# Compressed logits behind four slices of the recurrent inputs, and a reordered start and end of the first attention

## What is computed

```python
# first layer: h = rmsnorm(x) @ w_in, split into z, xbc, dt, q, k, v, z_sb, gates
y   = ssd_scan(silu(conv(xbc)), dt, ...)
for each block of 128 queries and each of 16 heads:          # stick-breaking
    logits   = (q @ k.T) / 8                                  # keys before the query
    log_fail = log_sigmoid(-logits);  between = suffix sums of log_fail
    o        = exp(log_sigmoid(logits) + between) @ v
merged = g_ssd * (gated_norm(y, z) @ w_ssd_proj) + g_sb * ((o * silu(z_sb)) @ w_sb_proj)

# second layer
q  = rms_norm(q) ; ks, kw = rms_norm(...) ; kc, vc = compress(...)   # 31 compressed keys
p_cmp = masked_softmax(q @ kc.T)      # compressed logits: need q and kc, not ks or kw
hi = h @ w_in_2[:, HI0:HI0+512]       # the recurrence's values
```

## Time and profile before

| | |
|---|---|
| median of 3 runs | 1399.78 us |
| profiled execution | 1397.56 us, its span 1395.8 us |
| PE busy | 1366.4 us, 98% of the span |
| DVE busy | 753.2 us, 54% |
| ACT busy | 608.8 us, 44% |
| mean clock granted to PE | 0.996 |
| moved by DMA | 121.27 MB, 87 GB/s |

### The profile page before, as it was taken

One profiled execution on the slowest core, in us unless ns is written; L12 is line 12 of the kernel. 1 busy time (PEld: TensorE's weight loads), 2 busy tenths in 40 slices (PEclk: granted clock), 3 DMA queues, 4 the chain that ended last, 5 costly groups with the idle time before them and its releaser, 6 DMA issues. The chain is left out here.

```text
span 1395.8 us, 18000 instructions
## 1 busy us (share of the span) xinstructions
PE 1366.4 (98%) x7055; PEld 1131.8 (81%) x7055; DVE 753.2 (54%) x1180; ACT 608.8 (44%) x1128; POOL 54.3 (4%) x38
## 2 busy tenths in 40 slices
PE   9999999999999999999998999999999999999999
PEld 7878778877888888887787777878898888888887
DVE  4875544456666554445557677668554433443333
ACT  5553333457777533223425467763343212321221
POOL 0015310000000000000010000000000000000000
PEclk9999999999999999999999999999999999999999
DMA  4222122242111244222441100101422332223223
GB/s 153 87 76 91 62 76 93 89 131 82 31 62 61 86 170 147 91 91 73 154 131 47 60 28 19 32 0 55 156 77 91 106 106 91 91 92 102 95 89 106
DMA packets 35349, 121.27 MB, mean 87 GB/s; under 512 B 3908, under 2 KB 5188, under 8 KB 35010
## 3 DMA queue, kind: packets, MB, share of 16 engines
q1 hardware_dynamic: 34690, 119.07, 26.0%
q10 hardware_dynamic: 576, 1.05, 0.3%
HBM read 112.77 MB, written 4.19 MB: 84 GB/s over the span
## 5 line engine op out<-in xcount | busy, mean ns | idle before, releaser
L845 PE MATMUL bank<-a_hi,whi 128*128 128x512 f32 (+1 forms) x880 | 346.3, 393 | 1.4 <-DVE arena L2108 0.9
L845 PE MATMUL bank<-a_hi,wlo 128*128 128x512 f32 (+1 forms) x880 | 336.9, 383 | 0.0
L845 PE MATMUL bank<-a_lo,whi 128*128 128x512 f32 (+1 forms) x880 | 336.4, 382 | 0.0
L1268 ACT ACTIVATE whi<-wraw 128x1024 fp32r<-128x1024 f32 x194 | 197.1, 1046 | 193.2 <-PE bank L845 169.3
L1620 DVE TENSOR_TENSOR wlo<-wraw,whi 128x1024 fp32r<-128x1024 f32 x194 | 238.2, 1239 | 61.6 <-ACT whi L1268 56.9
L845 PEld LDWEIGHTS bank<-a_hi,whi 128*128 128x128 f32 x880 | 165.8, 188 | 32.9 <-ACT whi L1268 2.0
L845 PEld LDWEIGHTS bank<-a_hi,wlo 128*128 128x128 f32 x880 | 165.5, 188 | 32.6
L845 PE MATMUL bank<-arena 128*128 128x128 f32 (+5 forms) x1332 | 185.1, 285 | 6.8 <-DVE arena L1982 2.6
L845 PEld LDWEIGHTS bank<-a_lo,whi 128*128 128x128 f32 x880 | 165.9, 188 | 30.6 <-issue 1.4
L845 PEld LDWEIGHTS bank<-arena 128*128 128x128 f32 (+1 forms) x1332 | 165.4, 191 | 18.7 <-issue 6.4
L845 PE MATMUL bank<-whi,a_hi 128*128 128x512 f32 x288 | 115.8, 402 | 2.4 <-DVE wlo L1620 2.3
(11 more groups left out here) (257 smaller groups left out, 1718.5 us busy)
## 6 DMA issues: line engine op xcount, KB each, us to landing
wraw<-in_wblk SPq DMA_DIRECT2D x190, 512.0 KB, 3.7
arena<-in_x SPq DMA_DIRECT2D x4, 512.0 KB, 6.1
arena<-in_x SPq DMA_DIRECT2D x1, 2048.0 KB, 7.6
spill<-arena SPq DMA_DIRECT2D x4, 512.0 KB, 7.7
arena<-spill SPq DMA_DIRECT2D x1, 2048.0 KB, 9.4
out<-arena SPq DMA_DIRECT2D x8, 256.0 KB, 2.6
arena<-arena SPq DMA_DIRECT2D x2, 896.0 KB
arena<-in_w1k SPq DMA_DIRECT2D x1, 1024.0 KB, 7.2
```

What stands on the lines that cost most here:

```text
L845: return nc.tensor.matmul(o, lhsT, rhs, start=start, stop=stop, **kw)
L1268: A(whi[n % 2][:, cols], wraw[i][:, 0:cols.stop - cols.start], ACT.Copy).then_inc(s_hi, 1)
```

## The change

It has seven edits, all of them in order and waits; the arithmetic is the same.

1. Two slices of `k` are put before the weave of the scan; the weave then holds two fewer.
2. The first four slices of `hi` come before the first compressed logits (one came before them until now).
3. `cmp(0, 0)` waits for query tile 3 instead of key tile 5; the wait for tile 5 is now at `cmp(0, 2)`.
4. The banks of `gate` and `y_ssd` go round as 1, 2, 0, not 0, 1, 2.
5. The second shifted copy of the values is issued behind the load of piece 1 of its block, not piece 0.
6. At the start of the first attention the logits no longer wait for all of the values to be copied (head 1's first product does). DVE writes the differences of half 0 before the stacks of head 0, and ACT takes one sigmoid of a single number after its part of the stacks, which loads its sigmoid table there.
7. `z_sb` tiles wait for the last head's output (`s_o`) only where they take bank 3.

```diff
@@ plan()
-    steps += weave([("ssd", c, part) for c in range(NT) for part in range(5)], kq)
+    steps += kq[:2] + weave([("ssd", c, part) for c in range(NT) for part in range(5)], kq[2:])
...
-    steps += weave(cmps, token("w_in_2", HI0, "hi", 0, "A"))
+    hi = token("w_in_2", HI0, "hi", 0, "A")
+    steps += hi[:4] + weave(cmps, hi[4:])
@@ plan_tiles()
-              "gate": (0, 1, 2), "y_ssd": (0, 1, 2)}
+              "gate": (1, 2, 0), "y_ssd": (1, 2, 0)}
...
-SHIFTS = [block_of("v") + 4, block_of("v") + 5]
+SHIFTS = [(block_of("v") + 4, 0), (block_of("v") + 5, 1)]
@@ SP
-                    if i == 0 and n in SHIFTS:
-                        half = SHIFTS.index(n)
+                    if (n, i) in SHIFTS:
+                        half = SHIFTS.index((n, i))
@@ PE, free_bank
-                if TILES[g][0] == "z_sb":
+                if TILES[g][0] == "z_sb" and BANK[g] == BANKS_STICK[1]:
                     pe.wait_ge(s_o, SH)
@@ PE, cmp
                     if qt == 0:
                         pe.wait_ge(s_vcd, 1)
-                        pe.wait_ge(*ended(tile_of("turn_qk", 5)))
+                        pe.wait_ge(*ended(tile_of("turn_qk", 3)))
...
                 if i == 2:
                     pe.wait_ge(s_cp, qt + 1)
+                    if qt == 0:
+                        pe.wait_ge(*ended(tile_of("turn_qk", 5)))
@@ PE, stick
                     if u == 0:
-                        pe.wait_ge(*end_sem("v"))
...
                     if qt == 0:
                         pe.wait_ge(s_dv, 1 + h // 8)
+                        if h == 1:
+                            pe.wait_ge(*end_sem("v"))
@@ ACT, ("stack",)
                         stack(0, i)
+                    A(unit_root, unit, ACT.Sigmoid)
@@ DVE, ("stack",)
-                    for i in range(2):
-                        stack(0, i)
                     for half in range(2):
                         link(v.memset(v_before[half][0:1, 0, :], 0.0))
                     for t in range(NT):
                         steps_of_values(0, t)
+                    for i in range(2):
+                        stack(0, i)
```

## The result

| | before | after |
|---|---|---|
| median | 1399.12 us (4 runs, 1397.88 to 1401.15) | 1385.75 us (4 runs, 1384.90 to 1386.26) |
| profiled execution | 1397.56 us | 1386.26 us |
| its span | 1395.8 us | 1384.5 us |

The ratio is 0.9902 (95% interval 0.9885 to 0.9920): 13.7 us faster by the ratio, 13.4 by the medians. Forecast were 12.4 us and 1387.4 us.

A forecast was written before the change was run, and what follows sets the result against it. PE was taken as the bound, busy 98% of the span; 3.47 + 3.23 + 1.37 + 3.43 + 0.88 = 12.38 us off the 1399.78 us median gave 1387.4 us, range 1384.0 to 1392.5 us.

The forecast's parts named there:

- Compressed logits, 3.47 us: Before the first compressed logits: PE's 3.47 us wait for the last turned tile's split goes; other end 0.
- clock, 3.23 us: Behind that idle time at 754 us: PE's clock stays up instead of 0.50 for 6.45 us, gaining 3.23 us.
- Either edit alone covers the 3.47 us: At the first compressed logits: the added hi slices or the relaxed tile wait would each remove the whole 3.47 us.
- Scan, 1.37 us: Start of the recurrent scan: two more k slices cover PE's 1.37 us wait for DVE's last convolution product.
- First attention, 3.43 us: Beginning of the first attention: three PE waits in a row give 3.43 us together; ends 0.89 and 3.62 us.
- (c): First attention, third wait, at 321.05 us: an earlier weight load lets ACT round sooner; 1.4 of 1.59 us taken.
- (b): First attention, second wait, at 317.10 us: ACT starts 2.29 us earlier; gain 1.14 us, 0.4 us to spare.
- Rival 2: First attention: ACT stays late, PE waits as before at the second and third place; 1389.9 us, chance 0.12.
- `z_sb`, 0.88 us: End of the first attention: z_sb(0) no longer waits for the last head's output copy; gain 0.88 us, other end 0.
- 1 (the clock falls among slices, transposes and 32-column matmuls all the same): Rival at the compressed logits: PE's clock falls even without the idle time, 3.23 us missing; 1390.6 us, chance 0.14.
- 3: Rival: each wait is followed by another ending as late, so the 754 us stall only moves; 1396.7 us, chance 0.07.
- 4: Rival in the scan's four chunks: DVE's moved L1620 holds the product PE needs; 7.2 us slower, 1407 us, chance 0.03.

The follow-up runs named there:

- table_back: The changed kernel without the early sigmoid of a single number, so the table loads at the first gate sigmoid; ran once, 1387.19 us.
- dve_back: The changed kernel with DVE's part of the stacks back ahead of the fills and value differences; ran once, 1385.24 us.
- cmp_both: The kernel before with only the compressed-logits edits (four hi slices ahead, first logits wait for query tile 3); ratio 0.9961, 1391.22 against 1398.32 us.
- without_cmp: The changed kernel with the edits at the compressed logits undone; ratio 0.9963, 1391.14 us.
- cmp_wait: The kernel before with the wait for query tile 3 alone, one hi slice ahead of the logits as before; ratio 0.9968, 1393.56 us.
- ends_back: The changed kernel with two PE waits put back: all values' copies before the first logits, last head's output before every z_sb tile; ran once, 1386.63 us.
- kq_back: The changed kernel with the scan's weave as it was, no slices put ahead of it; ran once, 1388.59 us.

## Why the prediction was right, point by point

**The mechanisms.** All six waits went, and none came back elsewhere as long. The time is 1.7 us below the forecast and the gain 1.0 us above it.

**The term that was mis-sized.** I took each wait at its idle time in the brackets. But a matmul's row ends later than the moment at which the next one can start, and how much later shows after, where nothing waits. PE's timeline after, the rows ahead of the scan's first product, of the attention's second late transposes and of `z_sb(0)`:

```profile
99.85 0.40 PE L846 MATMUL bank<-a_hi,wlo 128*128 128x512 f32 x1
...
313.38 0.23 PE L846 MATMUL bank<-cstb 128*128 128x128 bf16 x1
...
474.90 2.01 PE L846 MATMUL bank<-arena 128*128 128x128 f32 x14
```

The next rows start at 100.08, 313.58 and 476.67 us, which is 0.17, 0.03 and 0.24 us before the ends of these. The step that the engine loses to a wait is the idle time plus this overlap: by before's slightly shorter rows 0.16 us more at the scan and before the compressed logits, 0.15 at the first logits of the attention, 0.03 at each of its two late transposes, 0.24 at `z_sb(0)`, 0.77 us in all. The stretches bear it out, to 0.15 us: `z_sb(0)` gave 1.09 us against 0.88 + 0.24, the scan 1.68 against 1.37 + 0.16, the first attention 3.94 against 3.62 + 0.21; and where only transposes wait, the stretch grows by hardly more than what is shown (`table_back` 1.27 against 1.29, `dve_back` 1.66 against 1.52). With it the sum is 12.38 + 0.77 + 0.19 (the rest of the third wait) - 0.26 (the clock) = 13.1 us, against 13.37 by the stretches. The 0.26 is itself what the measured stretch leaves for the clock, so the sum tests the other terms and not that one.

**Compressed logits, 3.47 us, and clock, 3.23 us.** Right: 6.70 forecast, 6.60 by the stretch (3.47 + 0.16 of the wait leave 2.97 for the clock). By the times it is 7.1 us (`cmp_both`, medians; 5.5 by the ratio), or the 6.2 us that `without_cmp` falls short of the whole 13.4. "Either edit alone covers the 3.47 us" was the step that failed: I asked what PE waits for and not what stands behind the same split in DVE's order; `cmp_wait` shows the softmax there, and PE waiting for it. The clock's price was that of one execution. It recurs behind an idle time as long as this (three profiles of three at this place), but was about 6.5, 6.5 and 3.4 us long. That this term came so close is in part luck: it was read from one execution, and in `without_cmp` the same stretch costs 1.4 us less.

**Scan, 1.37 us.** Right, 1.68. (The weave holds 62 slices and held 64, not 60 and 62 as the prediction has it; the 0.1 slice stands.) The L1620 moved ahead of the scores' copy took 2.15 us on DVE beside GpSimd, near the 2.45 taken, and the product then waited for ACT, as argued (DVE's timeline after, lines answering to the earlier trace rows):

```profile
100.07 2.15 DVE L1625 TENSOR_TENSOR wlo<-wraw,whi 128x1024 fp32r<-128x1024 f32 x1 [1.23 <-ACT whi L1272]
102.14 0.41 DVE L2036 COPY arena<-bank 128x256 f32<-128x256 f32 x1
103.95 0.69 DVE L2041 TENSOR_TENSOR arena<-arena 128x512 f32<-128x512 f32 x1 [1.41 <-ACT arena L1584]
```

**First attention, 3.43 us.** Measured 3.94. DVE, ACT and SP after, answering to the earlier trace rows:

```profile
300.45 2.50 DVE L2088 TENSOR_TENSOR arena<-arena 128x512 f32<-128x512 f32 x4
303.46 0.68 DVE L2079 TENSOR_TENSOR rounded_arena<-arena,rounded_arena 64x512 fp32r<-64x512 f32 x1 [0.50 <-ACT rounded_arena L1392]
304.77 0.69 DVE L2082 TENSOR_TENSOR rounded_arena<-arena,rounded_arena 64x512 fp32r<-64x512 f32 x1 [0.63 <-ACT rounded_arena L1396]
305.49 1.23 DVE L1625 TENSOR_TENSOR wlo<-wraw,whi 128x1024 fp32r<-128x1024 f32 x1
```
```profile
304.75 1.28 ACT L1591 ACT_TABLE_LOAD   x1
...
308.25 0.27 ACT L1407 ACTIVATE arena<-bank 128x128 f32<-128x128 f32 x1
...
313.16 0.28 ACT L1417 ACTIVATE arena<-bank 128x128 f32<-128x128 f32 x1
313.46 1.06 ACT L1272 ACTIVATE whi<-wraw 128x1024 fp32r<-128x1024 f32 x1
```
```profile
299.27 7.79 SPq L791 DMA_DIRECT2D wraw<-in_wblk  x2
308.38 0.67 SPq L799 DMA_DIRECT2D arena<-arena  x1
```

The differences stand ahead of the stacks, the table load ahead of the sigmoids, the load ahead of the shift at 308.38 us, and ACT's rounding at 313.46 us waits for no DMA. Taking 1.4 of 1.59 us for (c) was needless caution: all of it went. That wait is also not a fixed one. In the six profiles with before's start of the attention it is 1.21, 1.32, 1.59, 1.87, 1.99 and 2.06 us, because it hangs on when a weight piece lands. For (b) I reckoned 0.4 us to spare; the chip has none to speak of (`table_back`). Rival 2 stood closer than its chance of 0.12 says.

**`z_sb`, 0.88 us.** Right, 1.09, shown by `ends_back` as well.

**Busy and idle time.** I named 3 us less busy and 9 less idle; the profiles show 5.1 and 6.2. The idle times removed sum to 9.34 us. Against them stand 0.93 us more in the first 21 us, where loads differ between executions, 1.08 us in two idle times at 660.82 and 664.89 us, which only a PE at full clock meets, and 1.21 us between 777.92 and 945.40 us. Of these about 0.9 are no idle time: the profile after lacks four matmul records (7051 of 7055), and `dve_back`, which has them all, shows no bracket and one of 0.71 us at the places where after shows 0.41 (819.10 us) and 1.03 (857.09 us). The rest is a wait of 0.34 us for ACT at 828.67 us. So PE's busy time really fell by some 4 us and its idle time by some 7. As to the two at 660.82 and 664.89 us, before ran at half clock for 3.4 us behind 665 us, and PE came late enough to wait for nobody. The 3.4 us at half clock there therefore cost little. From 659.46 to 747.51 us it took 88.05 us with it, and 87.99 without. In `kq_back`, where 6.8 us at half clock stand there, it took 89.92.

**The rivals.** 1 (the clock falls among slices, transposes and 32-column matmuls all the same): no; it stayed at 1.00 there in after and in all seven other kernels with the four slices, one profile of each. Only where an idle time stood there (`cmp_wait`) did it fall. 2: no, but narrowly. 3: for the slices no; `cmp_wait` is a small case of it. 4: no; the slow L1625 falls into DVE's idle time.

**Left open.** The 0.14 us of the scan; why the same idle time of 2.29 us halves the clock in six profiles and not in seven; what about 2 us would have done before the compressed logits.

## What to carry to other kernels

An idle time before a small product goes when independent work of the same list is put ahead of it; count the slices that really stand there in the order, for a weave may move one along. Relaxing the wait alone can leave a part of the idle time at the next thing that the other engine's order holds back (0.86 of 3.47 us here). A wait in a row of them can be worth more than its own row once those ahead of it are gone (3.2 us here, not 1.59), so take them away together and reckon each from the new times.

## What the runs showed of the hardware

- An idle time of PE costs more than the timeline shows, by as much as the next matmul would have overlapped the one before: about 0.16 us behind a 128x512 matmul (0.39 us shown, steps of 0.2265), 0.24 behind the 128x128 ones before `z_sb(0)`, but 0.03 where transposes follow a 128x128 bf16 one.
- The clock of PE fell from 1.00 to 0.50, for 3.4 or 6.8 us, behind all four idle times of 3.2 us and more, and behind shorter ones (0.86 us in `cmp_wait`, 1.5 to 2.3 us) in some executions only; behind none of 0.87 to 1.4 us after the first 21 us. So an idle time of PE has a second price, which changes from run to run: the two profiled executions of the kernel before spent about 10 and 17 us at half clock, leaving aside their ends.
- Mixed with transposes and 24- and 32-column matmuls, 128x512 matmuls kept the clock at 1.00.
